# Two-layer decoder trunk on one core: branch turns moved behind query turns, the last result in quarters, three stage boundaries rewritten

## What is computed

```python
for l in range(2):
    h = rms_norm(x, mix_norm_g[l])
    z = h @ w_in[l]
    y_a = gmlp_branch(z_u, z_v, ...) @ gm_w_proj[l]      # branch A: u * (W_s v + b)
    y_b = mla_branch(z_cq, z_ckv, z_kr, ...) @ mla_w_proj[l]   # branch B: attention, 16 heads
    gates = sigmoid(z_gates)
    x = x + (gates[0] * y_a + gates[1] * y_b) @ w_out[l]
    h2 = rms_norm(x, ffn_norm_g[l])
    if l == 0:
        x = x + (silu(h2 @ Wg) * (h2 @ Wu)) @ Wd           # dense feed-forward, 2816 wide
    else:
        x = x + moe_swiglu(h2, ...)                        # top 2 of 8 experts, 2816 wide each
```

## Time and profile before

| | |
|---|---|
| median of 3 runs | 1450.35 us (1450.29 to 1450.68) |
| the profiled execution | 1450.41 us, of which the span is 1448.7 us |
| PE / PEld busy | 1438.9 us (99%) / 1187.5 us (82%) |
| DVE / ACT busy | 1160.6 us (80%) / 964.0 us (67%) |
| granted TensorE clock | 1.00 in every stretch asked for |
| HBM | 398.20 MB read, 286 GB/s over the span |

### The profile page before, as it was taken

The page is one execution under the profiler, slowest core; times in us unless marked ns, Lnnn a source line. Parts: engine busy times, 40 slices in busy tenths (PEclk is TensorE's granted clock), DMA queues, the critical chain, the costliest instruction groups (busy, mean ns, idle before and its releaser), DMA issues.

```text
span 1448.7 us, 19542 instructions
## 1 busy us (share of the span) xinstructions
PE 1438.9 (99%) x6850; PEld 1187.5 (82%) x6850; DVE 1160.6 (80%) x1144; ACT 964.0 (67%) x1053; POOL 44.5 (3%) x53
## 2 busy tenths in 40 slices
PE   9999999999999999999999999999999999999998
PEld 7888788888888888878888888888888888888886
DVE  6977756665546977656998999999989899899997
ACT  6676754444435676754677777777777777777775
POOL 2000003000000000000200000000000000000300
PEclk9999999999999999999999999999999999999999
DMA  9473348955465463447799999999999999999995
GB/s 341 150 237 117 116 149 302 332 178 177 156 219 177 149 230 116 144 147 272 301 394 380 390 361 395 395 361 395 364 394 395 352 401 373 388 391 359 372 368 218
DMA packets 212316, 414.95 MB, mean 286 GB/s; under 512 B 14188, under 2 KB 55528, under 8 KB 212248
## 3 DMA queue, kind: packets, MB, share of 16 engines
q1 hardware_dynamic: 206232, 393.42, 75.0%
q0 software_dynamic: 4976, 16.97, 3.5%
q10 hardware_dynamic: 1040, 3.68, 0.6%
HBM read 398.20 MB, written 15.81 MB: 286 GB/s over the span
## 4 chain that ended last, share of the span: by engine, by line
PE 98%; ACT 1%; DVE 1%; DMA 0%; issue 0%; SPq 0%; ACTq 0%
PE ps L534 89%; PE ps L1083 1%; PE ps L957 1%; PE ps L935 1%; PE ps L795 1%; PE ps L944 1%; PE ps L915 1%; PE ps L934 0%; PE ps L884 0%; PE ps L1064 0%; DMA xres<-in_x 0%; ACT act_hi L1243 0%; PE ps L928 0%; PE ps L850 0%; PE ps L1075 0%; PE ps L913 0%
## 5 line engine op out<-in xcount | busy, mean ns | idle before, releaser
L504 DVE TENSOR_TENSOR w_lo<-raw,w_hi 128x2048 fp32r<-128x2048 f32 (+1 forms) x242 | 515.8, 2141 | 151.4 <-ACT w_hi L499 147.3
L499 ACT ACTIVATE w_hi<-raw 128x2048 fp32r<-128x2048 f32 (+2 forms) x241 | 433.6, 1801 | 215.2 <-PE ps L534 198.1
L534 PE MATMUL ps<-w_hi,act_hi 128*128 128x512 f32 (+1 forms) x1264 | 332.7, 393 | 1.3 <-ACT act_hi L1243 1.1
L534 PE MATMUL ps<-w_hi,act_lo 128*128 128x512 f32 (+1 forms) x1264 | 328.0, 388 | 0.0
L534 PE MATMUL ps<-w_lo,act_hi 128*128 128x512 f32 (+1 forms) x1264 | 325.0, 387 | 0.0
L534 PEld LDWEIGHTS ps<-w_lo,act_hi 128*128 128x128 f32 x1264 | 235.5, 188 | 48.8 <-DVE w_lo L504 0.5
L534 PEld LDWEIGHTS ps<-w_hi,act_lo 128*128 128x128 f32 x1264 | 235.0, 188 | 48.2
L534 PEld LDWEIGHTS ps<-w_hi,act_hi 128*128 128x128 f32 x1264 | 231.0, 188 | 47.0 <-ACT act_hi L1243 1.6
L499 ACT ACTIVATE w_hi<-raw_more 128x2048 fp32r<-128x2048 f32 x96 | 170.7, 1778 | 65.5 <-PE ps L534 64.0
L504 DVE TENSOR_TENSOR w_lo<-raw_more,w_hi 128x2048 fp32r<-128x2048 f32 x96 | 201.1, 2110 | 14.3 <-ACT w_hi L499 12.9
L504 DVE TENSOR_TENSOR w_lo<-raw_low,w_hi 128x2048 fp32r<-128x2048 f32 (+1 forms) x64 | 128.9, 2022 | 12.4 <-ACT w_hi L499 11.3
(11 more groups left out here) (286 smaller groups left out, 1278.7 us busy)
## 6 DMA issues: line engine op xcount, KB each, us to landing
raw<-in_moe_w_gu SPq DMA_DIRECT2D x192, 512.0 KB, 9.7
raw_more<-in_moe_w_gu SPq DMA_DIRECT2D x96, 512.0 KB, 10.0
raw<-in_w_in SPq DMA_DIRECT2D x72, 512.0 KB, 4.5
raw_low<-in_moe_w_gu SPq DMA_DIRECT2D x64, 512.0 KB, 9.6
raw_more<-in_moe_w_down SPq DMA_DIRECT2D x64, 512.0 KB, 6.2
raw<-in_dense_w_gu SPq DMA_DIRECT2D x44, 512.0 KB, 4.9
raw_low<-in_moe_w_down SPq DMA_DIRECT2D x32, 512.0 KB, 8.1
raw<-in_moe_w_down SPq DMA_DIRECT2D x32, 512.0 KB, 5.8
```

What stands on the lines that cost most here:

```text
L499: nc.scalar.activation(w_hi[:, self.split_slot(j), 0:n], self.raw(j)[:, 0:n], ACT.Copy).then_inc(self.hi, 1)
L504: nc.vector.tensor_tensor(w_lo[:, c, 0:n], self.raw(j)[:, 0:n], w_hi[:, c, 0:n].bitcast(F32), ALU.subtract).then_inc(self.lo, 1)
L534: return nc.tensor.matmul(dst, a, b, start=start and n == 0, stop=stop and n == 2)
```

## The change

Five edits.

- **Branch turns**: `a_turns` half 1 goes from inside `gb` 1, k 4 (cut 5) to inside `pa` 0, k 0 (cut 1), and `qk_turns` 3 and `norm_probs` 2 come one cut earlier.
- **First weights**: x's second row tile comes in two halves with semaphores of their own; DVE instead of ACT makes the first half of the first `w_hi`; the first `w_lo` is made in two halves; the first chunk goes through k-steps outermost, so that four matmuls instead of two need only the first half; 10 fillers instead of 20.
- **Dense feed-forward**: norm turns half 0 go inside the last `wo` chunk, half 1 inside the first `gu` chunk.
- **Change of layer**: the last `down` chunk is done in quarters, three of them, then norm turns half 0 of layer 1, then the fourth quarter; norm turns half 1 go inside the first chunk of layer 1; one split of weights on DVE goes behind the additions.
- **Last result**: one pass of the last down product changes place; its second half is scaled, spread, added and (its second row tile) stored in quarters of 256 columns, five stores instead of four.

```diff
-        plan.append(("norm_turns", l, 0, 0))
-        plan.append(("norm_turns", l, 0, 1))
-        if l:
-            plan.append(("split", l, len(chunks) - 1))
-        mul(l, "v", 0, 0, [("norm", l, 0)])
+        late = [("norm_turns", l, 0, 1), ("split", l, len(chunks) - 1)]
+        if not l:
+            plan.append(("norm_turns", l, 0, 0))
+            plan.append(("norm_turns", l, 0, 1))
+        mul(l, "v", 0, 0, [("norm", l, 0)], inside=[(5, step) for step in late] * (l > 0))
...
-            inside=[(2, ("exps", l, 2)), (5, ("a_turns", l, 1)), (6, turn(3)), (6, ("norm_probs", l, 2)),
+            inside=[(2, ("exps", l, 2)), (5, turn(3)), (5, ("norm_probs", l, 2)),
                     (6, split("split_hi"))])
         mul(l, "pa", 0, 0, [*slot(5, exps=False), split("split_lo"), ("softmax", l, 4)],
-            inside=[(4, turn(4)), (4, split("split_hi"))])
+            inside=[(1, ("a_turns", l, 1)), (4, turn(4)), (4, split("split_hi"))])
...
+        c = len(chunks)
+        routed_turns = [("norm_turns", l, 1, 0), ("squares", l, 1, 1), ("norm_turns", l, 1, 1), ("norm", l, 1, c)]
+        mul(l, "wo", 1, 4, [evac("wo", 1), ("squares", l, 1, 0)] + (routed_turns if l % 2 else [("squares", l, 1, 1)]),
+            inside=[(5, ("norm_turns", l, 1, 0))] * (l % 2 == 0), split=False)
         if l % 2 == 0:
             for j in range(GUS):
-                mul(l, "gu", j)
+                mul(l, "gu", j, inside=[(3, ("norm_turns", l, 1, 1)), (3, ("norm", l, 1, c))] * (not j))
...
-            plan.append(("down", l, a, len(chunks), strip_no, DOWN_CUT, len(DOWN_K)))
+            plan.append(("down", l, a, len(chunks), strip_no, DOWN_CUT, len(DOWN_K) - 1))
+            plan.append(("down_end", l, a, len(chunks), strip_no, 0))
+            plan.append(("norm_turns", l + 1, 0, 0))
+            plan.append(("down_end", l, a, len(chunks), strip_no, 1))
...
-        END_ORDER = ((0, 0, (0, 1, 2)), (0, 1, (0, 1)), (1, 0, (0, 1, 2)), (0, 1, (2,)), (1, 1, (0, 1, 2)))
+        END_ORDER = ((0, 0, (0, 1, 2)), (0, 1, (0, 1)), (1, 0, (0, 1)), (0, 1, (2,)), (1, 0, (2,)), (1, 1, (0, 1, 2)))
+        LAST = ((0, 0, 512), (1, 0, 512), (0, 512, 1024), (1, 512, 768), (1, 768, 1024))
...
-            for t in range(TT):
-                sp.dma_start(xres[:, t, :], x[0, t * P:(t + 1) * P, :]).then_inc(x_landed[t], 16)
+            sp.dma_start(xres[:, 0, :], x[0, 0:P, :]).then_inc(x_landed[0], 16)
+            for h in (0, D // 2):
+                sp.dma_start(xres[:, 1, h:h + D // 2], x[0, P:2 * P, h:h + D // 2]).then_inc(
+                    x_landed[1] if h else x_half_landed, 16)
...
-                        keep_busy(20)
+                        keep_busy(10)
...
-                        if not c and at == 2:
+                        if not c and at == 4:
                             pe.wait_ge(hi_done, 1)
...
+                elif kind == "down_end":
+                    a, n, part = step[2], *step[4:6]
+                    last, kt = a + len(DOWN_K) - 1, DOWN_K[-1]
+                    ...
+                    for hf, t in ((0, 0), (0, 1), (1, 0)) if not part else ((1, 1),):
+                        for p in range(3):
+                            ...
+                        mm.then_inc(chunk_used if part else down_half, 1)
...
-                    pe.wait_ge(z["y_half1"], 1)
                     for t in range(TT):
-                        nc.tensor.matmul(ps[:, 2 + t, :], put[:, t * P:(t + 1) * P], y_sb[:, 512:1024], start=True, stop=True
-                                         ).then_inc(z["scattered"], 1)
+                        for quarter, ready in enumerate((z["y_half1"], z["y_end"])):
+                            if not t:
+                                pe.wait_ge(ready, 1)
+                            c = 256 * quarter
+                            bank = (2, 2, 3, 4)[2 * t + quarter]
+                            nc.tensor.matmul(ps[:, bank, c:c + 256], put[:, t * P:(t + 1) * P],
+                                             y_sb[:, 512 + c:768 + c], start=True, stop=True).then_inc(z["scattered"], 1)
...
-                            act.wait_ge(first_landed, 16)
-                            copy(w_hi[:, 0, 0:CHUNK // 2], ring.raw(0)[:, 0:CHUNK // 2]).then_inc(first_hi, 1)
                             act.wait_ge(raw_landed[0], 16)
                             copy(w_hi[:, 0, CHUNK // 2:CHUNK], ring.raw(0)[:, CHUNK // 2:CHUNK]).then_inc(hi_done, 1)
...
-                        copy(y_sb[:, 512:1024], ps[:, 7, :], slot_w[:, 0:1]).then_inc(z["y_half1"], 1)
+                        copy(y_sb[:, 512:768], ps[:, 7, 0:256], slot_w[:, 0:1]).then_inc(z["y_half1"], 1)
+                        copy(y_sb[:, 768:1024], ps[:, 7, 256:512], slot_w[:, 0:1]).then_inc(z["y_end"], 1)
...
+            dve.wait_ge(first_landed, 16)
+            nc.vector.tensor_copy(w_hi[:, 0, 0:CHUNK // 2], ring.raw(0)[:, 0:CHUNK // 2]).then_inc(first_hi, 1)
+            dve.wait_ge(first_hi, 1)
...
+                    for i, (hf, t) in enumerate(((0, 0), (0, 1), (1, 0)) if not part else ((1, 1),)):
+                        if part:
+                            dve.wait_ge(chunk_used, b)
+                        else:
+                            dve.wait_ge(down_half, 3 * (l // 2) + i + 1)
+                        cols = slice(hf * STRIP, (hf + 1) * STRIP)
+                        op = tt(xres[:, t, cols], xres[:, t, cols], ps[:, (2 * n + 2 * t) % 4 + hf, :], ALU.add)
+                        op.then_inc(strip_free[(n + t) % 2] if hf else x_summed, 1)
+                    if part:
+                        splits(b - 2, b - 1)
```

More of the change, by code:

```diff
@@ L827, in _ @@
                     banks = [turn_bank(b0), turn_bank(b0 + 1)]
+                    if (l, step[2], half) == (0, 0, 1):
+                        pe.wait_ge(x_landed[1], 16)
                     if (l, step[2], half) == (0, 0, 0):
@@ L981, in _ @@
                             wait_turns_split(operand + 1)
-                        if p == 2 and not cell:
+                        if p == 2 and not cell and not c:
+                            pe.wait_ge(first_lo, 1)
+                        if p == 2 and cell == (0 if c else 4):
                             ring.take_lo(pe, 0, c)
-                        t, k = divmod(cell, kt)
+                        t, k = divmod(cell, kt) if c else divmod(cell, TT)[::-1]
                         kk = k_at + k0 + k
@@ L1029, in _ @@
                             turn4(b0, lambda k, t: hid[:, (GUS - 1) % 2, t, k * P:(k + 1) * P])
+                elif kind == "down_end":
+                    a, n, part = step[2], *step[4:6]
+                    last, kt = a + len(DOWN_K) - 1, DOWN_K[-1]
+                    if not part:
+                        wait_turn_read(pe, last_turn["hidden_turn", l, GUS - 2] + 1)
+                    ch, cl = ring.take(pe, 0, last)
+                    for hf, t in ((0, 0), (0, 1), (1, 0)) if not part else ((1, 1),):
+                        for p in range(3):
+                            if p == 2:
+                                ring.take_lo(pe, 0, last)
+                            for k in range(kt):
+                                kk, c = KF - kt + k, k * D + hf * 512
+                                mm = one_pass(p, ps[:, (2 * n + 2 * t) % 4 + hf, :], hid_hi[:, kk, t * P:(t + 1) * P],
+                                              hid_lo[:, kk, t * P:(t + 1) * P], ch[:, c:c + 512], cl[:, c:c + 512],
+                                              False, kk == KF - 1)
+                        mm.then_inc(chunk_used if part else down_half, 1)
             pe.wait_ge(router_ready, 1)
@@ L1283, in _ @@
                         continue
+                    if not l:
+                        act.wait_ge(x_half_landed, 16)
                     for t in range(TT):
@@ L1702, in _ @@
                     if not l and not step[2]:
-                        for n in range(1, LEAD) if step[3] else (0,):
-                            ring.split_lo(dve, 0, n, size[n])
+                        if not step[3]:
+                            half = CHUNK // 2
+                            tt(w_lo[:, 0, 0:half], ring.raw(0)[:, 0:half], w_hi[:, 0, 0:half].bitcast(F32),
+                               ALU.subtract).then_inc(first_lo, 1)
+                            dve.wait_ge(hi_done, 1)
+                            tt(w_lo[:, 0, half:CHUNK], ring.raw(0)[:, half:CHUNK], w_hi[:, 0, half:CHUNK].bitcast(F32),
+                               ALU.subtract).then_inc(lo_done, 1)
+                        else:
+                            for n in range(1, LEAD):
+                                ring.split_lo(dve, 0, n, size[n])
                 elif kind == "latent_norm":
@@ L2009, in put_part, with last_scattered @@
                     op.then_inc(z["put_ready"], 1)
+                def last_scattered():
+                    for i, (t, c0, c1) in enumerate(LAST):
+                        dve.wait_ge(z["scattered"], (1, 2, 4, 5, 6)[i])
+                        if not c0:
```

(5 more changed lines are left out.)

70 lines of the change are left out of this document (26 added, 44 removed).

## The result

| | before | after |
|---|---|---|
| median | 1450.64 us (6 runs, 1450.29 to 1452.91) | 1456.35 us (6 runs, 1455.49 to 1458.47) |
| ratio, with its 95% interval | | 1.004 (1.003 to 1.005) |
| the profiled execution | 1450.41 us, span 1448.7 | 1455.49 us, span 1453.8 |

The changed kernel is slower by 0.4%, 5.7 us on the medians. The forecast was 1452.6, with 1455.9 as the top of its range: the time lies 3.8 us above the forecast and 0.45 above the range.

The account below looks back on a forecast made before the run. PE, busy 99% of the span, was taken to bound the kernel. The terms 4.9 - 0.5 - 0.8 - 1.05 - 0.3 = +2.25 us on 1450.35 gave 1452.6 us, own range 1451.0 to 1454.0, 8-in-10 range 1450.4 to 1455.9.

Parts of the forecast that it names:

- What bounds the kernel: Whole kernel: PE is busy 99% of the span, so edits elsewhere count only through PE idle time removed or made.
- Branch turns, what goes (0.7 a layer): In the chunk before `pa` 0, PE's 0.70 us idle, mostly for `t_lo`, goes; `pa` 0 starts at 151.9.
- Branch turns, what comes: At the query turns in `pa` 0, PE waits 3.2 us for DVE's late `t_lo`: +4.9 us net for both layers.
- rival 2: At the query turns, `t_lo` comes before PE needs the banks, so no new wait: 1446.2 us, chance 0.11.
- First weights (-0.5): At the start, `hi_done` comes at 10.1 instead of 10.35 with four matmuls already done: -0.5 us (-0.8 to -0.1).
- Dense feed-forward (-0.8): Between `wo` and `gu`, 0.74 us of PE idle and some refill go: -0.8 us (-0.9 to -0.3).
- Both thin margins: In `gu` and layer 1's first chunk, PE's work covers the half 1 turns' inputs by only 0.3 to 0.4 us.
- rival 3: Hidden turns in `gu` and layer 1 come late, so -1.85 us shrinks to -0.8: 1453.7 us, chance 0.11.
- Change of layer (-1.05): Between `down` and layer 1, 1.43 us of PE idle shrinks to a 0.37 wait: -1.05 us (-1.4 to -0.6).
- Last result (-0.3): At the end, the last addition ends at about 1444.1, set by DVE's additions: -0.3 us (-0.8 to +0.1).
- Sum and forecast: Whole kernel: all terms add to +2.25 us on the median of 1450.35, giving 1452.6 us; chance 0.66.
- rival 1: The new wait at the query turns drops PE's clock, slowing matmuls behind it, 2.8 us in all: 1455.4 us, chance 0.12.

Follow-up runs that it names:

- the split behind: Changed kernel with DVE's split of weights and normalising of pair 3 moved behind `t_lo`: 1446.93 us, run again 1447.07.
- the two kernels that change nothing else: Changed kernel with only DVE's normalising moved behind `t_lo`, 1450.76 us; with its split of weights moved as well, 1446.93 us.
- The three experiments on the end: Four stores instead of five with the branch edit undone, 1448.46 us, and with the split behind, 1446.60; the last-result edit undone with the split behind, 1447.49.
- The filled wait: Changed kernel with 12 more matmuls that add zero, just ahead of the query turns of pair 4 in both layers: 1453.81 us.
- longer wait: Changed kernel with the query turns of pair 4 six matmuls earlier in `pa` 0, so PE waits 4.2 us: 1459.75 us.

## Why the prediction was wrong, point by point

**What bounds the kernel: right.** Only PE's idle time counted, and it was at the named places.

**Branch turns, what goes (0.7 a layer): right.** `pa` 0 starts at 151.12, where 151.9 less the 0.69 of the start was forecast. The version with the split behind keeps this part alone and is 1.5 us faster than the one without the branch edit.

**Branch turns, what comes: right.** The wait at line 972, twice, ended by line 1642, was forecast at 3.2 us and measured at 2.86 (`t_lo` was forecast to start at 157.8, which is 157.1 once the 0.69 gained at the start is taken off, and starts at 157.06); the net loss was forecast at +4.9 and is 2 x 2.39 in the trace and +4.75 in the undisturbed runs of the branch edit alone. That DVE's order (split, normalising, then `t_lo`) sets it is shown by the two kernels that change nothing else: 2.86 us becomes 1.68, then 0. One reading under rival 2 is off: for no wait `t_lo` has to come earlier by the whole length of the wait (1.18 us earlier took 1.18 off it), 3.2 us by the forecast's own figures and not 2.3. It didn't come, so nothing hung on it.

**First weights (-0.5): right on average.** -0.69 in the first trace, 0.44 over all of them, 0.6 between the medians. The load bounds it, as said: `hi_done` was forecast at 10.1, and ACT's copy of the second half runs from 9.05 to 10.11.

**Dense feed-forward (-0.8): right**, -0.79. Both thin margins held, so rival 3 did not come.

**Change of layer (-1.05): right**, -0.99.

**Last result (-0.3): the addition right, the gain not shown.** The last addition was to end at about 1444.1 instead of 1444.44. Measured from the same matmuls, it ends 0.31 us earlier. All of this is its own shorter length; it starts at the same distance (8.54 and 8.57 us). The step that failed is that this would reach the end of the span: the stretch behind it, issue and landing of the last store, took 0.41 us more in this trace. The three experiments on the end could not tell 0.3 from nothing.

**Sum and forecast: wrong by the one term that was not in it.** Without the clock the sum, +2.25, is close to what the traces give, +2.4. The step that failed is that the sum puts the clock's part at nothing and leaves it to rival 1. Its mechanism was named as it came: an idle time of this length, matmuls 0.43 us apart behind it (3.20 us for eight in the rows above). Two things in it were mis-sized. The first is its chance, 0.12. "No wait of PE in the trace is near 3.2 us" was taken as evidence against it, though it only said that the trace could not tell; and the earlier trace rows showed that PE does run at half its pace behind an idle start. The clock fell in three of the four waits of 2.9 us that were profiled (one of two in the changed kernel, two of two with the branch edit alone), and by the mean clocks, 0.996 to 0.998, all six runs of the changed kernel had at least one fall. The second is its price. The rule for it, half of the time spent at the low level, is close to what the runs show, but the length was borrowed from the start of the program, 2.4 us, which is only the length of the row of twelve fillers (in the changed kernel's trace the slow pace of the start lasts until about 6.7: eight transposes from 4.98 on are 0.22 us apart); here PE worked for 2.8 to 6.0 us at the low level, and one fall cost 1.2 to 2.7 us where 1.2 to 1.6 was forecast. With the fitting chance, rival 1 would have been the forecast: 1452.6 plus one or two falls is 1454 to 1458, and 1456.35 was measured. The filled wait shows that this is most of the difference: without a fall the loss is +3.06 us instead of +5.7. The remaining 0.8 us above the forecast's +2.25 (0.2 by the other way of adding up) are not the clock; the scatter of the start can hold a part of them, and the rest is not explained.

The prediction cited the Trainium skill, "TensorE: Matmul & The Clock Gate", section "Why this matters for your kernels", on gaps between bursts of matmuls. No row spoke for it then. The windows of the changed kernel do so in layer 0, 0.50 for 6.8 us around the end of a gap of 2.86; in layer 1, with the same gap, the clock stayed at 1.00.

## What to carry to other kernels

A step moved on the engine that bounds the kernel is only as early as the slowest of its partners: before moving a turn, read which operations stand ahead of it on the engine that frees its bank, and move those with it; here two steps moved on DVE turned +5.7 us into -3.8. Price a new idle time of PE that is longer than those of the trace (here 1.7 us did no harm and 2.9 did) twice, once as a delay and once as a possible fall of the clock in it or behind it. The sign to look for is the mean clock of each run beside its time: 0.995 to 0.998 in thirteen of the fifteen runs with waits of 2.9 or 4.2 us, and 0.999 or 1.0 in all runs of the other versions but one (1449.09 us with 0.998, the slowest of the nine with the split behind and four stores; it has no trace). The spread of the times alone is no sign: 3.0 us in the changed kernel, but 0.7 in the version with 4.2-us waits, and 0.8 to 3.6 in versions without a fall. If such a wait can't be avoided, work that changes nothing in it (here twelve matmuls that add zero) kept the clock.

## What was not expected of the hardware

- The same wait, 2.86 to 2.87 us, let the clock fall in three cases and not in the fourth. At 1.68 us it never fell (twenty waits), at 4.2 always (eight waits), as far as the runs' times and clocks tell. What decides in between was not found.
- The low stretches of the five falls that were traced come in two lengths: 3.4 us three times (branch edit alone, both layers; longer wait, layer 1) and 6.8 us twice (changed kernel and longer wait, both layer 0).
- A fall doesn't begin at a fixed distance from PE's last matmul. It began 2.1 us into the idle time in the changed kernel (157.1) and 2.2 in layer 1 of the branch edit alone (592.7); 2.7 and 4.1 us into it with the longer wait; and in layer 0 of the branch edit alone a microsecond after PE had resumed (159.3). At the end of the program, where PE has nothing left to do, the clock fell 2.2 us after its last matmul in the changed kernel, and had not fallen 5.0 us after it, when the span ended, in the kernel before. So a new wait is not safe because a wait or an idle end of that length did no harm in one trace.
- The start of DVE's copy of the first weights, which waits for their load, scatters by 0.7 us between ten traces with the same start (7.78 to 8.48), more than the edit of the start gains on average.
